# Where x and the second part's arrays start in SBUF: 128 instead of 64 bytes from the weights modulo 256

## The reference, cut to what matters

```
x = x + 0.5 * swiglu_ffn(rmsnorm(x, g1), w_gu, w_down)      # D_FF = 2816
x = x + ab_mixer(...)   or   nsa_mixer(...)
x = x + 0.5 * swiglu_ffn(rmsnorm(x, g2), w_gu, w_down)
```

```
proj = modulate(rmsnorm(x)) @ w_in
x = x + g1 * ((sigmoid(g_pool) * pool + sigmoid(g_ret) * ret) @ w_out)
act = gelu(hb . u[eidx]);  out = (softmax(best) * act) . v[eidx]   # top 16 of 16384, 8 heads
```

## Time and profile before

| | |
|---|---|
| median of 3 runs | 2109.06 us |
| profiled execution, its own time | 2114.19 us |
| profiled execution, span | 2112.3 us |
| instructions | 39282, of them 15850 matmuls |
| PE busy | 2086.9 us, 99% |
| PE weight loads busy | 1961.5 us, 93% |
| POOL, ACT, DVE busy | 78%, 53%, 42% |
| granted TensorE clock | 0.998 of full speed |

### The profile page before, as it was taken

How to read it: one execution, slowest core, us unless ns; L and a number is a source line. 1 busy time by engine, 2 the same in 40 slices (tenths; PEclk the granted TensorE clock), 3 DMA queues, 4 the chain that set the end, 5 groups by cost and what they waited for, 6 DMA issues and landing times.

```text
span 2112.3 us, 39282 instructions
## 1 busy us (share of the span) xinstructions
PE 2086.9 (99%) x15850; PEld 1961.5 (93%) x15850; DVE 883.0 (42%) x1922; ACT 1111.8 (53%) x1782; POOL 1642.1 (78%) x812
## 2 busy tenths in 40 slices
PE   9999999999999998999999999999999999999998
PEld 9999889999999977999889999999999998888886
DVE  7113634113111564311655316996677512222224
ACT  6454765435434455544654545555555555555555
POOL 4887677887888766888756676798667789999997
PEclk9999999999999999999999999999999999999999
DMA  8555666556555432555453354454444455555554
GB/s 308 198 180 199 259 240 249 189 198 253 198 194 189 180 135 81 205 196 199 172 182 140 145 180 185 134 189 161 148 142 145 147 180 199 192 197 190 195 193 150
DMA packets 77297, 391.60 MB, mean 185 GB/s; under 512 B 10716, under 2 KB 11868, under 8 KB 46816
## 3 DMA queue, kind: packets, MB, share of 16 engines
q1 hardware_dynamic: 77152, 389.61, 52.1%
HBM read 388.52 MB, written 1.05 MB: 184 GB/s over the span
## 4 chain that ended last, share of the span: by engine, by line
PE 72%; POOL 6%; issue 3%; DVE 3%; ACT 1%; DMA 0%; POOLq 0%; ACTq 0%; DVEq 0%
PE bank L480 22%; PE bank L481 22%; PE bank L482 22%; POOL ring_low L421 6%; PE bank L2698 3%; PE bank L966 2%; POOL nsa_SB L1685 0%; PE bank L1776 0%; DVE nsa_hidR L1959 0%; PE bank L1803 0%; PE bank L1821 0%; DMA ring_raw<-in_stream 0%; DVE nsa_SB L2016 0%; DVE nsa_Sc L1985 0%; DVE keep_red L2405 0%
## 5 line engine op out<-in xcount | busy, mean ns | idle before, releaser
L421 POOL TENSOR_TENSOR ring_low<-ring_raw,ring_high 128x2048 fp32r<-128x2048 f32 x201 | 930.4, 4641 | 320.7 <-ACT ring_high L407 319.6
L2658 POOL TENSOR_TENSOR peerS_low<-peerS_raw,peerS_high 128x512 fp32r<-128x512 f32 x510 | 659.4, 1310 | 116.4 <-ACT peerS_high L2801 115.6
L480 PE MATMUL bank<-keep_xThigh,ring_high 128*128 128x256 f32 x2080 | 583.4, 280 | 1.4 <-DVE keep_xTlow L2963 0.5
L481 PE MATMUL bank<-keep_xTlow,ring_high 128*128 128x256 f32 x2080 | 577.6, 278 | 0.0
L482 PE MATMUL bank<-keep_xThigh,ring_low 128*128 128x256 f32 x2080 | 577.5, 278 | 0.0
L407 ACT ACTIVATE ring_high<-ring_raw 128x2048 fp32r<-128x2048 f32 x204 | 391.0, 1917 | 284.2 <-PE bank L482 243.7
L2801 ACT ACTIVATE peerS_high<-peerS_raw 128x512 fp32r<-128x512 f32 x510 | 319.6, 628 | 168.8 <-PE bank L482 157.3
L480 PEld LDWEIGHTS bank<-keep_xThigh,ring_high 128*128 128x128 f32 x2080 | 390.8, 188 | 9.4 <-issue 6.7
L482 PEld LDWEIGHTS bank<-keep_xThigh,ring_low 128*128 128x128 f32 x2080 | 392.4, 189 | 0.0
L481 PEld LDWEIGHTS bank<-keep_xTlow,ring_high 128*128 128x128 f32 x2080 | 391.1, 188 | 0.3
L480 PE MATMUL bank<-keep_xThigh,peerS_high 128*128 128x256 f32 x1024 | 292.0, 285 | 0.0
(11 more groups left out here) (557 smaller groups left out, 3571.2 us busy)
## 6 DMA issues: line engine op xcount, KB each, us to landing
ring_raw<-in_stream SPq DMA_DIRECT2D x235, 1024.0 KB, 4.8
peerS_raw<-in_experts SPq DMA_DIRECT2D x256, 512.0 KB, 3.6
start_x<-in_x SPq DMA_DIRECT2D x2, 512.0 KB, 4.2
ring_raw<-in_stream SPq DMA_DIRECT2D x4, 256.0 KB, 5.4
context_in<-in_ctx SPq DMA_DIRECT2D x1, 1024.0 KB
mix_band_band<-in_band SPq DMA_DIRECT2D x1, 1024.0 KB, 7.2
peerT_keys_keys<-in_stream SPq DMA_DIRECT2D x1, 1024.0 KB, 5.0
out<-keep_x SPq DMA_DIRECT2D x4, 256.0 KB, 2.2
```

What stands on the lines that cost most here:

```text
L421: self.nc.gpsimd.tensor_tensor(low_, self.raw_slot(n), high.bitcast(F32), ALU.subtract).then_inc(self.low_done.sem, 1)
L480: mm(out, sh, mh, start=start, stop=False)
L481: mm(out, sh, ml, start=False, stop=False)
L2658: g_.tensor_tensor(low[:, m % 2, cut], xraw[:, m % 3, cut], high[:, m % 2, cut].bitcast(F32), ALU.subtract).then_inc(made_low.sem, 1)
```

## The change

Three constants are changed. `keep` goes 64 bytes down, and with it everything that stands there. In `second` and in `peer`, arrays that are placed at 16 kB or more behind `ring_end` go 64 bytes down too (128 less than the round offset instead of 64); the largest array of PEER and its last expert row, which end at `keep` in the order of that stage, follow it.

```diff
 def sbuf_plan(nc):
     ring_end = base + (RAW + 2 * SPLIT) * TILE * 4
-    keep = end - (3 * 8192 + 4256)
+    keep = end - (3 * 8192 + 4256 + 64)
...
     def second(self):
...
         def at(name, kb, cols, dt=F32):
-            return Arena(nc, f"mix2_{name}", self.ring_end + 1024 * kb - 64 * (kb >= 16), self.keep)(name, cols, dt=dt)
+            return Arena(nc, f"mix2_{name}", self.ring_end + 1024 * kb - 128 * (kb >= 16), self.keep)(name, cols, dt=dt)
...
     def peer(self):
...
-        at = lambda name, kb, cols: Arena(nc, f"peerT_{name}", self.ring_end + 1024 * kb - 64 * (kb >= 16), self.keep)(name, cols)
+        at = lambda name, kb, cols: Arena(nc, f"peerT_{name}", self.ring_end + 1024 * kb - 128 * (kb >= 16), self.keep)(name, cols)
```

## The result

The changed kernel is slower: 2143.17 us (median of 4 runs, 2143.06 to 2145.51) against 2108.95 us (4 runs, 2107.89 to 2114.75), a ratio of 1.0162, 95% interval 1.015 to 1.0175. The forecast was 2091 us. The range of 2085 to 2139 us missed the time by 4 us, and the nearest of the cases was rival C (slow everywhere, 2132 to 2138 us).

What follows compares the result with a forecast made beforehand. TensorE, busy 99% of the span, was taken to bound the kernel through the distance between matmul starts. Terms of -9.5, -9.4, -2.2, +2.9, -1.4, +1.1 and 0 gave -18.5 us off 2109.1: 2090.6 us, range 2085 to 2139.

Steps and rivals of the forecast that it cites:

- rival C: All products at 128 bytes slow: +23 us for x, up to +6 for h, 2132 to 2138 us; chance 0.21.
- forecast A: At 128 bytes moving columns and weight loads don't meet, all moved products fast: 2090.6 us, 2086 to 2099; chance 0.42.
- x over the ring and the expert rows: 6240 and 3072 products of 256 columns, 34% and 68% slow, all become fast: -9.5 and -9.4 us.
- two upper readings: Bounds for the 9312 x products: +23 us if all are slow, +44 us if all take the gait of distance 0.
- The second part: Its 480 mixed-array products, all slow at 281 ns, become fast: -2.2 us.
- h: Unmoved feed-forward hidden values take over the gait of the x before: -1.4 us, or +6.2 if x is slow.
- 88 changes of distance: Each feed-forward changes distance twice in a group, about 12 ns a change: +1.1 us.
- x as weights: 384 products under 512 moving columns: 0.8 us back or as much again or twice lost; taken as 0.
- Rival D: The streams' meeting place recurs every 128 bytes, so 128 equals 0: +45 us, about 2154 us; chance 0.15.
- Rival B: Still two gaits with shares about as now, or in strong form no effect of placement: 2103 to 2116 us; chance 0.22.
- a weight load that is held up has room: At 512 moving columns a delayed weight load has room; at 256 it holds up the next matmul.
- the loads of 48 columns: Support for the weight-load reading: with x moving as elsewhere, these products have 276 ns.

Runs made afterwards that it cites:

- Experiment 1: Bare TensorE products without the kernel's computation, moving columns at eight distances from the weights modulo 256: 113.3 to 120.0 ns between starts at 256 columns.
- the second part alone: Against the kernel before, only the second part's mixed arrays move to 128 bytes, x stays: 2108.35 us, ratio 0.999.
- x alone: Against the kernel before, only x and what stands behind it moves, the second part's arrays stay: 2140.99 us, ratio 1.014.
- Experiment 3: Bare products with low halves placed apart, or six products at another distance ahead of 36 at 192: 113.35 ns with low weights shifted by 128 bytes.
- the second version of experiment 6: Against the kernel before, low weights of the ring and of PEER's first 128 expert rows lie 128 bytes from the high ones: 2097.32 us, ratio 0.9941.

## Why the prediction was wrong

**The failed step** is the choice of forecast A: "at 128 bytes the streams don't meet, all fast". It rested on one trend, from 0 bytes (283 ns) to 64 below (276 in more than half), drawn on to the farthest distance. Experiment 1 shows that there is no such trend: 120.0, 116.7, 117.8, 119.9, 118.7 or 120.0, 117.3, 113.3 or 117.8, 118.3 ns. The short gait is a property of 192, not of being far away. The prediction held the counter-evidence itself, 64 above at 280 ns in the earlier trace rows, and gave it a line under "against".

**x over the ring and the expert rows.** Put at -9.5 and -9.4 us; measured +27.3 and +8.7. The slow shares of 34 and 68% that the first two terms took away were read correctly (excess 9.2 and 8.9 us), but nothing of them went, and the fast share became slow as well. The prediction's own two upper readings hold it between them: +23 us if all were at 117.8 ns, +44 if all were at 120, measured +36. Rival C had the right sum in another division, so its closeness is in part luck: +23 for x and up to +6 for h, where the profiled executions have +36 for x, +0.5 for the second part, -2.8 for h and -4.7 for the wait in the nsa mixer and small groups, +29 both times. That its 2138 us ends 5 us short of the median is the base: a price read from an execution 5.1 us above the median was added to the median.

**The second part.** Put at -2.2, measured +0.5 in the full change and +0.5 in the trace of the second part alone. Its 480 products were slow before, and 128 bytes has much the same price; in x alone, where they stay at 192 behind x at 128, they gain the 2.1 us. The term was right in size for a change that left them alone.

**h.** -1.4 was put on "it takes over the gait of the x before it", +6.2 if x became slow. x became slow and h fast, -2.8 us in sums. So the step fails, and that its sign came true is luck. Experiment 3 has the rule in its place: the change of distance settles the gait, and 128 into 192 gave fast in all four entries, which the second part repeats in x alone. The 1.1 us for 88 changes of distance don't show; the excess of h after is 0.4 us in all.

**x as weights.** Taken at 0 between -0.8 and twice that upward. Start to start it rose from 229 to 232 ns (medians of 384), 1.2 us, inside the bounds. The sum fell all the same, by 2.3 us, since TensorE has less to wait for in the nsa mixer: it comes there 13.1 us later than before, and what it waits for 11.2 us later. The windows of before show what such a wait costs beside itself: behind it nine records in 3 us, at half the clock. The wait on this line was 2.3 us before; the waits of after have

```profile
PE bank L1776 <- DVE nsa_kT L1939: 0.4, 1, 0.4
```

and before, 761.5 to 764.5 us, against four microseconds later:

```profile
761.50:764.50 3.00, 3.00 (x9) 0.51 0.51 216
766.00:770.00 4.00, 4.00 (x24) 1.00 0.00 0
```

**What held.** No engine but TensorE decides, no new wait came, the time moved with the x groups. 1370 to 1430 us lost four records where A gained, and the search stayed hidden. Rival D's rule, a period of 128 bytes, falls: at 512 columns 0 has 226.7 ns and 128 233.5 or 232.1, at 256 columns 0 never had the 118.7 ns that two of the four bare runs at 128 had, and the time is 11 us under its 2154. Rival B's strong form falls too. The Trainium skill, "TensorE: Matmul & The Clock Gate", section "Step-by-step: what each phase is for", gives TensorE two independent read ports on SBUF. The prediction's reading of it, that placement would change nothing, is refuted by 113.3 to 120.0 ns for the same bare instruction, by start address alone. Only B's weak form is true, and only for 192: which of its two gaits runs is drawn at each interruption, and the 10 us between the executions of before (2104.69 to 2114.75 in the runs of this study) are probably that draw. Only one of those executions has a trace; but in that of the second part alone, 6.4 us shorter, x and h stand at unchanged addresses and have 5.6 us less excess. At 128 four runs lie within 2.5 us.

**The picture behind it.** The prediction said that at 512 columns a weight load that is held up has room. The bare runs have 226.7 to 234.1 ns there, 7.4 between the places, against 6.7 at 256 columns, so that step fails too. Its support from the loads of 48 columns was weak: their 276 ns is what 128 columns have at 192 in the fast gait. And POOL's 4.7 us for a tile divides the busy time of one window by the count of the other; 81.8 / 18 and 83.7 / 19 are 4.5 and 4.4, which changes nothing.

What makes the streams cost each other time modulo 256 stays open. The runs show the price of each place, and that the third product's weights matter, not the structure behind it. That two streams meet, as the prediction has it, is not shown.

## What to carry to other kernels

Where TensorE is busy throughout and the same instruction has two durations in different stretches, look at the operands' start addresses modulo 256 before anything else, and measure the price of a place by bare products in the kernel's own order of operands; don't draw a line through two of them. The place that is best for 256 moving columns isn't that for 512, so arrays with both uses want two addresses. And read the cost of a state that is drawn anew in each execution from several executions, or take it off the one in which it was read.

## What the runs showed of the hardware

- A product with 128 columns of fp32r weights and 256 moving columns starts every 113.3 to 120.0 ns at 2.4 GHz, with 512 columns every 226.7 to 234.1 ns, by the moving start less the weights' start modulo 256, measured over weights at 128. At 256 columns, distances of 256 and 512 bytes more are the same.
- At distance 192 two gaits are stable, 113.3 and 117.8 ns, over hundreds of products at a stretch (80 to 180 us of before has 117.8, 900 to 1000 us 113.3); which one is settled by what runs just ahead. At 128 there are two as well, 118.7 and 120.0 ns, both without the short one.
- With the low weights 128 bytes from the high ones, and moving columns at 192 from the high ones, 113.3 ns ran behind every entry, seven of seven bare runs, and in the kernel 1.5 us of excess were left in 6240 products. Over the same weights, moving columns at 64 from the high ones had it too, four of four.
- A wait of TensorE of 1.9 us, once, was followed by half the granted clock (0.50 over 3 us, 13 products at 213 ns). In before a wait of 2.3 us was followed by seven starts 427 ns apart; in the second version of experiment 6 one of 2.6 us at the same place wasn't.
